# Re-placing the small work of a hybrid backbone step: gate halves, modulation rows, merge inputs, expert prologue, scatter to the outputs

## The reference, cut to what matters

```
mod = silu(c) @ w_mod + b_mod                      # 12 chunks of 512: sh1 sc1 g1 sh2 sc2 g2
h = rms_norm(x) * (1 + sc1) + sh1
hq, hff, hfb, hi, hg, dq, dk, dv, gl = split(h @ w_in)
o_h = bidirectional gated linear recurrence(hq, hff, hfb, hi) per head, rms-normed, * silu(hg)
o_a = softmax(q1 k1) v - lam * softmax(q2 k2) v per head, rms-normed
merged = sigmoid(gl_h + b) * (o_h @ w_bh) + sigmoid(gl_a + b) * (o_a @ w_ba)
x = x + g1 * (merged @ w_out)
h = rms_norm(x) * (1 + sc2) + sh2
x = x + g2 * experts(h)     # 16 experts, each takes its 64 best latent and 16 best context rows
```

## Time and profile before

| | |
|---|---|
| median of 3 runs (lowest to highest) | 1557.84 us (1555.29 to 1558.34) |
| the profiled execution, its own time | 1554.0 us |
| its span | 1552.2 us |
| PE busy, mean granted clock | 1361.0 us (88%), 0.916 |
| DVE, ACT, POOL busy | 1017.9, 704.6, 254.3 us |
| share of the chain of waits: PE, DVE, ACT, issue, DMA | 68, 16, 6, 6, 2% |

### The profile page before, as it was taken

How to read it: one execution, slowest core, us unless ns; L and a number is a source line. 1 busy time by engine, 2 the same in 40 slices (tenths; PEclk the granted TensorE clock), 3 DMA queues, 4 the chain that set the end, 5 groups by cost and what they waited for, 6 DMA issues and landing times.

```text
span 1552.2 us, 18203 instructions
## 1 busy us (share of the span) xinstructions
PE 1361.0 (88%) x6827; PEld 1012.6 (65%) x6827; DVE 1017.9 (66%) x1091; ACT 704.6 (45%) x674; POOL 254.3 (16%) x161
## 2 busy tenths in 40 slices
PE   6888988899698989785998986899999999999993
PEld 1577877788687879662787743566666666666662
DVE  1765134452776868672325465899889999889992
ACT  2322234443343535322212104666667667666761
POOL 1021001110000000000000000124431324444411
PEclk9899989899699999858989877999999999999997
DMA  9403201113103121316006337899999999999993
GB/s 363 139 26 130 83 9 45 49 36 113 58 1 99 46 89 53 105 59 240 27 1 232 122 137 281 295 361 354 381 368 371 376 357 377 366 359 374 374 354 85
DMA packets 111666, 298.67 MB, mean 192 GB/s; under 512 B 6853, under 2 KB 32837, under 8 KB 111561
## 3 DMA queue, kind: packets, MB, share of 16 engines
q1 hardware_dynamic: 108344, 286.87, 50.9%
q0 software_dynamic: 3264, 11.01, 3.1%
HBM read 281.09 MB, written 19.40 MB: 194 GB/s over the span
## 4 chain that ended last, share of the span: by engine, by line
PE 68%; DVE 16%; issue 6%; ACT 6%; DMA 2%; POOL 1%; DVEq 0%; SPq 0%; ACTq 0%; POOLq 0%
PE ps L1528 17%; PE ps L1529 17%; PE ps L1530 17%; PE ps L1594 4%; PE ps L1698 4%; DVE w_lo L1458 3%; ACT w_hi L1011 2%; DVE w_lo L1056 1%; ACT w_hi L832 1%; PE ps L1649 1%; ACT arena L836 1%; DVE arena L1474 1%; DMA arena<-in_w_mod_dram 1%; DMA arena<-in_w_out_dram 1%; PE ps L1773 1%
## 5 line engine op out<-in xcount | busy, mean ns | idle before, releaser
L1458 DVE TENSOR_TENSOR w_lo<-arena,w_hi 128x2048 fp32r<-128x2048 f32 x192 | 435.4, 2287 | 63.3 <-ACT w_hi L1011 51.6
L1528 PE MATMUL ps<-w_hi,act_hi 128*80 128x512 f32 (+1 forms) x1048 | 419.1, 400 | 36.5 <-DVE w_lo L1458 22.8
L1529 PE MATMUL ps<-w_lo,act_hi 128*80 128x512 f32 (+1 forms) x1048 | 414.3, 395 | 0.0
L1530 PE MATMUL ps<-w_hi,act_lo 128*80 128x512 f32 (+1 forms) x1048 | 413.1, 394 | 0.0
L1011 ACT ACTIVATE w_hi<-arena 128x2048 fp32r<-128x2048 f32 x180 | 343.2, 1915 | 143.6 <-PE ps L1530 143.6
L1528 PEld LDWEIGHTS ps<-w_hi,act_hi 128*80 128x80 f32 (+1 forms) x1048 | 168.6, 161 | 122.7 <-DVE w_lo L1458 29.5
L1530 PEld LDWEIGHTS ps<-w_hi,act_lo 128*80 128x80 f32 (+1 forms) x1048 | 168.4, 161 | 75.5 <-issue 1.2
L1529 PEld LDWEIGHTS ps<-w_lo,act_hi 128*80 128x80 f32 (+1 forms) x1048 | 168.9, 161 | 69.0 <-issue 1.1
L1528 PE MATMUL ps<-act_hi,w_hi 128*128 128x320 f32 x576 | 189.6, 329 | 5.3 <-DVE act_lo L1363 5.3
L1529 PE MATMUL ps<-act_lo,w_hi 128*128 128x320 f32 x576 | 183.5, 319 | 0.0
L1530 PE MATMUL ps<-act_hi,w_lo 128*128 128x320 f32 x576 | 183.1, 318 | 0.0
(11 more groups left out here) (189 smaller groups left out, 1344.5 us busy)
## 6 DMA issues: line engine op xcount, KB each, us to landing
arena<-in_w_exp_gate_dram SPq DMA_DIRECT2D x64, 1024.0 KB, 8.8
arena<-in_w_exp_up_dram SPq DMA_DIRECT2D x64, 1024.0 KB, 7.2
arena<-in_w_exp_down_dram SPq DMA_DIRECT2D x64, 1024.0 KB, 6.8
arena<-in_w_mod_dram SPq DMA_DIRECT2D x24, 1024.0 KB, 6.4
arena<-in_w_in_dram SPq DMA_DIRECT2D x18, 1024.0 KB, 5.4
arena<-in_w_in_dram SPq DMA_DIRECT2D x12, 512.0 KB, 4.5
gl_raw<-arena SPq DMA_DIRECT2D x32, 160.0 KB, 1.8
arena<-gl_raw SPq DMA_DIRECT2D x8, 640.0 KB, 8.0
```

The costliest lines, as they stand in the source:

```text
L1458: v.tensor_tensor(Wl[sl], eraw[slot], Wh[sl].bitcast(F32), ALU.subtract).then_inc(s_el, 1)
L1528: t.matmul(out, sh, mh, start=start, stop=False)
L1529: t.matmul(out, sh, ml, start=False, stop=False)
L1530: return t.matmul(out, sl, mh, start=False, stop=stop)
```

## The change

All that is computed stays the same. Steps move in `STEPS`, and pieces move with them in `PIECES`.

- Attention: gate halves 0 to 19 now stand after steps -1 to 18 (before: 1 to 20), and halves 20 and 21 after steps 20 and 21. Splits stand after steps 2, 4, 8, 12, 16 and 19 (before: 2, 6, 10, 14, 18).
- Ahead of head 0: halves 22, 23 and modulation chunk 6 fill the place between the first projections and `pre`. Only one split (f1) is left there of three.
- Heads: the next head's half projections stand after levels 1 to 6 (before: 0 to 5). Head 0 has three gate halves, head 1 one half and chunk 7, head 2 two halves and chunk 8, head 3 two halves between its levels. Head 3's three splits leave its levels; two of them stand at `states` and `o`, one in the merge. Chunk 9 moves from ahead of head 3's `states` to behind its `sq`, chunk 4 behind `oT`.
- Merge: its input is split row by row in new steps `("ol", kt)`: the attention rows behind `sq` of head 3, the recurrence rows behind its `oT`. The attention product is made first. The broadcast of g1 is a step of its own, `("modg", j)`, and uses two banks: for chunk 4 it stands behind merge step 0; chunk 5 moves behind the merge, its broadcast between the halves of the output projection.
- Experts, prologue: the first three weight pieces are split ahead of the first rows; expert 1's rows are turned after piece 4, its splits go to buffers of their own (`xh1`, `xl1`), and `turn_a(0)` stands behind two pieces of expert 1.
- Experts, scatter: x is stored to the outputs themselves, and each expert's rows are added there by two indirect DMAs, 64 rows to `y_sample`, 16 rows to `y_prompt`. The last copies are gone. Two more index tables are made on DVE and PE, and POOL copies two index columns per expert.

```diff
-        for n in range(NI + 2):
+        at_half = {n: n + 1 for n in range(-1, 19)} | {20: 20, 21: 21}
+        for n in range(-1, NI + 2):
             STEPS.append(("da", n))
             if n in at_da:
                 split(*at_da[n])
-            if 1 <= n <= 20:
-                half(n - 1, 3)
-                drain(n - 1)
+            if n in at_half:
+                half(at_half[n], 3)
+                drain(at_half[n])
...
+        STEPS += projections(0)[0:2] + [("f", 0, 0)] + projections(0)[2:4] + [("f", 0, 1)] + projections(0)[4:6]
+        STEPS += [("fa", 0, 0), ("fa", 0, 1)]
         split("f", 1)
...
+        STEPS.append(("q", 0))
+        half(22, 2)
+        half(23, 2)
+        drain(22)
+        drain(23)
+        STEPS += [("mod", 6), ("pre", 0), ("diag", 0)]
+        LEVEL_SPLITS = {(0, 2): ("q", 1), (0, 4): ("gl", 6), (1, 1): ("f", 2), (1, 4): ("q", 2), (2, 0): ("gl", 7), (2, 1): ("f", 3), (2, 4): ("q", 3)}
...
-                if todo:
+                if todo and lv:
                     STEPS.append(todo.pop(0))
...
+                if lv == 0 and h == 0:
+                    STEPS.append(("modc", 6))
+                if h == H - 1 and lv in (2, 4):
+                    half(29 + lv // 2, 0)
...
+            if h in (1, 2):
+                STEPS += [("mod", 6 + h), ("modc", 6 + h)]
+            if h == H - 1:
+                split("br", 1, 0)
             STEPS.append(("states", h))
...
+        STEPS.append(("sq", H - 1))
+        STEPS += [("ol", kt) for kt in range(4, 8)]
+        STEPS += [("mod", 9), ("oT", H - 1)]
+        STEPS += [("ol", kt) for kt in range(4)]
+        STEPS += [("modc", 9), ("mod", 4)]
         for c in range(8):
             STEPS.append(("mrg", c))
+            if c == 0:
+                STEPS.append(("modg", 4))
+            if c == 1:
+                split("br", 1, 1)
             if c == 3:
-                split("br", 1, 1)
+                split("br", 0, 1)
                 split("out", 0, 0)
-                STEPS.append(("mod", 5))
...
+        STEPS.append(("mod", 5))
+        split("out", 0, 1)
+        split("out", 1, 0)
+        STEPS += [("out", 0, 0), ("modg", 5), ("out", 0, 1)]
+        split("out", 1, 1)
+        STEPS += [("out", 1, 0), ("out", 1, 1)]
...
             for i in range(NT):
                 sp.wait_ge(s_x1, NT + i + 1)
-                sp.dma_start(y_rows[i * P:(i + 1) * P, :], x1[:, i, :]).then_inc(s_yrow, 16)
+                sp.dma_start(y_tile[i], x1[:, i, :]).then_inc(s_yrow, 16)
...
-            sp.wait_ge(s_scat, 16 * NE)
-            sp.dma_start(y_prompt[0], y_rows[0:NCTX, :]).then_inc(s_yout, 16)
-            sp.dma_start(y_sample[0], y_rows[NCTX:T, :]).then_inc(s_yout, 16)
+            sp.wait_ge(s_scat, 32 * NE)
...
-                g.indirect_dma_start(out=y_rows, out_offset=bass.IndirectOffsetOnAxis(ap=iscat[0:CAP, 0:1], axis=0),
-                                     in_=ye[0:CAP, :], in_offset=None, compute_op=ALU.add).then_inc(s_scat, 16)
-                pool.wait_ge(s_scat, 16 * e + 16)
+                g.indirect_dma_start(out=y_sample[0], out_offset=bass.IndirectOffsetOnAxis(ap=iscat[0:CAP_LAT, 0:1], axis=0),
+                                     in_=ye[0:CAP_LAT, :], in_offset=None, compute_op=ALU.add).then_inc(s_scat, 16)
+                g.indirect_dma_start(out=y_prompt[0], out_offset=bass.IndirectOffsetOnAxis(ap=iscatc[0:CAP_CTX, 0:1], axis=0),
+                                     in_=ye[CAP_LAT:CAP, :], in_offset=None, compute_op=ALU.add).then_inc(s_scat, 16)
+                pool.wait_ge(s_scat, 32 * e + 32)
...
+                elif k == "ol":
+                    kt = st[1]
+                    if kt == 4:
+                        filled(act, ("gl", 15, 1))
+                        act.wait_ge(s_oa, NI)
+                    if kt < 4:
+                        act.wait_ge(free[3], USE["oT", kt][2])
+                    a.activation(act_hi[:, kt, :], (oh, oa)[kt // 4][:, kt % 4, :], ACT.Copy).then_inc(s_oth, 1)
...
+            for n in range(NHL):
+                elo(n % NHL, n + 1, n % NRE)
             xmod(0)
             xlo(0)
-            for n in range(8):
+            for n in range(NHL, 8):
                 elo(n % NHL, n + 1, n % NRE)
-            xmod(1)
-            xlo(1)
-            hidden(0, 8)
+                if n == 6:
+                    xmod(1)
+            xlo(1, (xh1, xl1))
...
             for n in range(8):
                 piece_mm(n // 4, n + 1, n % NHL, xh, xl, n % 4)
-            pe.wait_ge(s_xgm, 1)
-            turn_x(1)
-            pe.wait_ge(s_xgm, 2)
-            turn_a(0)
+                if n == 4:
+                    pe.wait_ge(s_xgm, 1)
+                    turn_x(1)
```

More of the change, by code:

```diff
@@ L47, in fused_step @@
     x_tile = [A["x_prompt"][0]] + [A["x_sample"][0, i * P:(i + 1) * P, :] for i in range(4)]
+    y_tile = [y_prompt[0]] + [y_sample[0, i * P:(i + 1) * P, :] for i in range(4)]
     with ExitStack() as ctx:
@@ L295, in fused_step @@
         head_pieces(0)
[L296 to L297 removed]
+        for h in range(H - 1):
             gl_piece(5 + h)
+            head_pieces(1 + h)
             mod_pieces(6 + h)
[L300 to L302 removed]
+        br_piece(1, 0)
         br_piece(0, 0)
[L304 to L305 removed]
         mod_pieces(9)
@@ L308, in fused_step @@
         br_piece(1, 1)
+        br_piece(0, 1)
+        out_piece(0, 0)
+        out_piece(0, 1)
         mod_pieces(5)
-        for n in range(2):
-            for s in range(2):
-                out_piece(n, s)
+        out_piece(1, 0)
+        out_piece(1, 1)
         order = [k for k, _, sp in PIECES if sp]
@@ L861, in _ @@
                         evac(G2s[0:CAP, 512 * (j - 10):512 * (j - 9)], ("g2", j), src=bank(4)[0:CAP, :])
+                elif k == "modc":
+                    if st[1] == 6:
+                        evac(mrow[0:2, :], ("modrow", 6), src=bank(2 * modpair(6))[0:2, :])
+                elif k == "modg":
+                    j = st[1]
+                    for c in range(2):
+                        evac(G1[:, c, 512 * (j - 4):512 * (j - 3)], ("g1", j, c), src=bank(2 * modpair(j) + c))
                 elif k == "xT":
@@ L1018, in _ @@
                 a.activation(Wh[n % NHL], eraw[n % NRE], ACT.Copy).then_inc(s_eh, 1)
-            act.wait_ge(s_eu, 4)
-            a.activation(aa[0:CAP, :], pair(0)[0:CAP, :], ACT.Silu).then_inc(s_silu, 1)
-            xhi(1)
+            filled(act, ("out", 1, NT - 1))
+            for n in range(NHL):
+                ehi_first(n)
+            xhi(0)
+            for n in range(NHL, 8):
+                ehi_first(n)
+                if n == 6:
+                    act.wait_ge(s_eu, 4)
+                    a.activation(aa[0:CAP, :], pair(0)[0:CAP, :], ACT.Silu).then_inc(s_silu, 1)
+            xhi(1, xh1)
             body(1)
@@ L1369, in _ @@
                     dve.wait_ge(s_sig, c + 1)
+                    filled(dve, ("my", c))
+                    release(v.tensor_tensor(halves(mt[1]), as2(pair(USE[("my", c)][0])), halves(gate[:, 8 + c, :]), ALU.mult), ("my", c))
+                    read(("my", c))
                     filled(dve, ("mx", c))
@@ L1372, in _ @@
                     read(("mx", c))
-                    filled(dve, ("my", c))
-                    release(v.tensor_tensor(halves(mt[1]), as2(pair(USE[("my", c)][0])), halves(gate[:, 8 + c, :]), ALU.mult), ("my", c))
-                    read(("my", c))
                     for b in ("mx", "my"):
@@ L1489, in body @@
                     elo((j + 2) % NHL, e * 12 + (j - 3), (j + 2) % NRE)
+                    if j == 1 and first:
+                        hidden(0, 8)
                     if j == 3:
@@ L1750, in _ @@
                     c = st[1]
-                    for b in range(2):
+                    for b in (1, 0):
                         if c == 0:
-                            pe.wait_ge(s_otl, 4 * b + 4)
+                            pe.wait_ge(s_otl, 8 - 4 * b)
                         key = ("br", b, c // 4)
@@ L1818, in body @@
                         pe.wait_ge(s_silu, e)
+                    if j == 2 and first:
+                        pe.wait_ge(s_xgm, 2)
+                        turn_a(0)
                     if j == 4:
```

179 lines of the change are left out of this document (85 added, 94 removed).

## The result

| | before | after |
|---|---|---|
| median of 19 runs (lowest to highest) | 1555.29 us (1551.63 to 1558.34) | 1559.91 us (1557.89 to 1562.45) |
| ratio to before, 95% interval | 1 | 1.0029 (1.0022 to 1.0037) |
| span of the profiled execution | 1552.2 us | 1560.4 us |
| mean granted clock | 0.916 | 0.917 |

The forecast was 1484, with a range from 1466 to 1511. The result lies 76 us over it, and on the other side of no change.

What follows compares the result with a forecast made beforehand. The PE-busy expert stage, DMA share 1.00, keeps its cadence; gains come from its ends and earlier stages. Terms +5.9 -26.8 -8.4 -24.2 -11.0 -9.4 sum to -73.9 us: 1484 from the median 1557.84, own range 1470 to 1498.

Steps and rivals of the forecast that it cites:

- Heads: -27 us: Heads 0 to 3: moved projections, gate halves, chunks and splits shorten each head's path over DVE; sum -26.8 us, bounds -12 and -34.
- state products that come sooner: Heads 0 to 2: with half and chunk gone ahead of them on PE, state products come 4.0, 3.5 and 3.5 us earlier.
- its two halves hidden in PE's 13 idle us: Head 3: its two gate halves fit into PE's idle time, so the head gains 6.5 us.
- Rival A: Waits eat half: ACT serves drains, exponentials and splits in one queue, some forty moved steps late; about 1511 us, chance 0.18.
- Up to head 0: Attention and the way to head 0: costs +5.9 us, projections start later, first level of head 0 near 422.
- Merge: Merge stage: without chunk 5 and its waits it takes 61.1 us instead of 80.3, -19.2 us.
- Output projection: Output stage: takes in chunk 5 and its broadcast, growing from 60.7 to 65.8 us, +5.1 us.
- Scatter and end: End of the experts: last copies go, second scatter adds its 1.41 us issue; -9.4 us, bounds -10.9 and -6.
- Rival C: End of the kernel: accumulating writes to the outputs land later, or the second scatter waits a full landing; 1493 us, chance 0.05.
- The rival of a slower loop (D): Expert loop: two indirect DMAs per expert make POOL's loop the bound; 1598 us, chance 0.04.
- Prologue: Start of the experts: earlier weight splits let PE start and reach piece 8 sooner; -11.0 us, bound 0.
- rival B: Start of the experts: weight loads set the pace, so the prologue's 11 us are not gained; 1495 us, chance 0.07.

Runs made afterwards that it cites:

- b_late: Kernel before with only the next head's half projections moved behind levels 1 to 6 instead of 0 to 5; 1591.65 us, ratio 1.0242.
- flate: Changed kernel with the sigmoid drains of the projections one level later (behind levels 4 and 6), PE's order untouched; 1519.31 us, ratio 0.9778.
- proj0: Changed kernel with half projections back behind levels 0 to 5 and splits of f2, f3 back ahead of level 0; 1523.54 us, ratio 0.9799.
- best2: Changed kernel with projections back, head 3's drains later, and in heads 1 and 2 oT ahead of the first half projection, f3 ahead of gl7; 1497.03 us.
- h3drain: Changed kernel with head 3's drains of gate halves 30 and 31 moved behind level 5 and behind prep; 1548.92 us, ratio 0.9950.
- hybrid: Kernel before up to head 3's last level (without splits in head 3's levels), changed kernel from there on; 1503.05 us, ratio 0.9670.
- best: Changed kernel with projections and f2, f3 splits back, head 3's drains later, store of half 27 behind the load of q3; 1508.60 us, ratio 0.9697.

## Why the prediction was wrong

**The step that failed is "Heads: -27 us".** It costed the moved projections as a gain ("-1.8 for PE's levels running free", "-2.6 (oT no longer behind a projection)") by PE's clearance and DVE's chain. It did not ask who drains them. Its -20.3 us for heads 0 to 2 became +40.5, because ACT's queue stood still behind the drain and DVE behind ACT. `b_late` shows the price of that alone: +36 us. `flate` and `proj0` show it in the changed kernel: -41 and -36. The prediction did ask for the queue of other moved steps (POOL's chain with two scatters, the load of chunk 6's second piece behind f1), but not for that of the drain, which was left where it stood while its producer moved.

A second term of that step was too large as well. It took 4.0, 3.5 and 3.5 us off for state products that come sooner. DVE waited for them 6.46, 6.49 and 6.49 us before, 3.98, 3.55 and 3.55 in the changed kernel, and 3.98, 5.49 and 5.40 in `best2`.

**Head 3** failed by the same thing: "its two halves hidden in PE's 13 idle us" was true of PE, and their drains cost 11 us over ACT (`h3drain`).

**Rival A** named the place (drains, exponentials and splits in one queue on ACT) and priced it as some forty waits of a micro-second each. It was eight waits of DVE of 4.4 to 8.6 us, two a head, 58.9 us in all, and one of 8.34 us for the log in head 0 (4.08 in the earlier trace rows), where ACT first drains half 24. The cost was not spread over the moved steps: it lay where an instruction without slack stood behind the drain. The evidence against A, that DVE's chain was counted row by row, was not evidence; the rows of before hold no wait that the new order makes.

**What held.** Up to head 0: first level at 418.9 (predicted near 422). That is in part luck, two misses that offset each other: attention did not end 7 us late (the projections start at 377.9, as before), and from there to level 0 it took 41.0 us instead of 36.6. From chunk 9 behind `o` of head 3 (751.48) to the merge: 15.1 us (predicted 15.6). Merge 62.9 (61.1), with one wait of 0.74 us for a split at 804.66, as the term had it. With the drains mended, head 3 to the merge took 66 us (`h3drain`, `best2`) and 67.1 (`hybrid`), where 90.5 - 25.0 = 65.5 was predicted, and heads 0 to 2 took 71.2, 72.0 and 73.7 (66, 72 and 71). `best2` comes nearest to the arithmetic of the prediction, with the drains mended and `oT` and f3 moved besides. By its span it gains 56.2 us of 73.9; of the 17.7 that are missing 8 are in heads 0 to 2 (5.2 of them in head 0), 3.4 at the end, 2.9 in the output stage, 2.0 in the prologue and 1.8 in the merge; smaller terms offset each other.

**Output projection** grew by 8.0 us and not by 5.1. The broadcast of chunk 5 takes 4.1 us (4.0 priced), chunk 5 its 7.0, and the wait of 3.85 us is gone. PE is busy for all of the 68.7 us: the 2.2 us credited for a cold start and for split stalls did not come; the 0.7 that then remain were not followed.

**Scatter and end**: -6.0 in the trace, the far bound. The second landing comes 5.4 us after the first scatter's issue, where one scatter took 5.2 before, so it adds 0.2 us and not 1.41; the 4.7 us behind it, which the prediction put at nothing, make the miss. Rival C asked for scatters that land later, and they do not. The rival of a slower loop (D) did not come: +1.1 us over 13 turns. In the changed kernel's loop the second scatter is issued 5.2 us after the first, and GpSimd goes on 12.9 us after the first, exactly as before:

```profile
1148.61 4.92 POOL L815 DMA_INDIRECT out_dram<-arena  x1 [11.05 <-DVE arena L1524]
1153.83 2.05 POOL L817 DMA_INDIRECT out_dram<-arena  x1 [0.30 <-issue]
1161.54 0.18 POOL L804 COPY arena<-arena 80x1 uint32 x1 [5.66 <-DMA out_dram<-arena]
```

The second landing lies beside the first. The fixed part of about 2.0 us per DMA issued by GpSimd, for which the prediction named the Trainium skill (DMA: Bandwidth & Descriptors, Anatomy of one DMA), is not seen as an added wait here.

**Prologue**: the turn of expert 2's rows comes 7.9 us sooner, not 11.0 (8.3 to 10.6 in the other runs with this prologue, so rival B, which gives 0, is out). The gather's rows arrive 8.5 us after its issue instead of 6.8 (953.60 to 962.12, and before 932.68 to 939.52), at a time when no weight split has to wait for them any more, so PE starts with the rows and no longer with the weights. That is 1.7 of the 3.1 us. Behind its first product PE is busy without a gap up to the turn, 42.8 us, where the prediction's terms leave 41.2:

```profile
962.12 1.30 PE L1846 MATMUL ps<-arena 80*128 80x80 f32 x8 [9.54 <-DMA arena<-xn_rows,arena]
966.90 0.71 PE L1571 MATMUL ps<-w_hi,act_hi 128*80 128x512 f32 x1 [3.47 <-DVE act_lo L1509]
```

## What to carry to other kernels

When a producer moves in one engine's order, find its drain in the other engine's queue, and ask what stands behind the drain and how much slack that has; the slack is read from the trace as the gap between the end of the queued work and its first use, here 0.1 us. A wait seen in the old trace only bounds what is there now; for each wait that the new order can make, a fair first price is the whole delay times how often it occurs, not a small allowance. And a change in many parts is best timed in parts: here one condition cost 36 us and the two drains of head 3 another 11, and together they hid the 47 us that `best` shows.

## What the runs showed of the hardware

A wait of PE is followed by work at the lower clock. Head 1 has 397 matmuls in the changed kernel and 396 in `best2`; they keep PE busy for 66.72 us at a granted clock of 0.84 in the one, and for 59.56 us at 0.93 in the other. In the changed kernel a level of 20 matmuls takes 4.50 us after a wait of 2 to 9 us and 2.34 when PE was kept busy, close to the ratio of the clock's two levels, 1.2 and 2.4 GHz:

```profile
521.18 4.53 PE L1747 MATMUL ps<-arena 128*128 128x64 f32 x20 [9.22 <-DVE arena L1333]
530.75 2.34 PE L1747 MATMUL ps<-arena 128*128 128x64 f32 x20
...
546.34 4.50 PE L1747 MATMUL ps<-arena 128*128 128x64 f32 x20 [3.93 <-DVE arena L1191]
```

What stayed open: what the 4.7 us behind the last scatter's landing are, and how much of the heads' loss in the changed kernel is the lower clock and how much the waits themselves, since no run kept the one without the other.
